# Dilated heads: values for four heads at once with tokens on partitions, and a head's outputs issued behind the gate's tile

## What is computed

```python
qb = rope(qb.reshape(B, S, hb, HEAD_DIM))          # hb = 3 groups * 4 heads
kb = rope(kb.reshape(B, S, hb, HEAD_DIM))
vb = vb.reshape(B, S, hb, HEAD_DIM)
yb = dilated_mixture(qb, kb, vb).reshape(B, S, W_B_OUT) * jax.nn.silu(zb)
# dilated_mixture: causal attention for each group with its window and dilation,
#   (128, 1), (512, 4), (2048, 16), and over the groups a softmax of their log-sum-exps:
w = jax.nn.softmax(jnp.stack(lses, axis=0), axis=0)
out = jnp.sum(w[..., None] * jnp.stack(outs, axis=0), axis=0)
```

## Time and profile before

| | |
|---|---|
| three runs | 3171.05, 3172.30, 3174.02 us (median 3172.3) |
| the profiled execution | 3171.53 us, of which its span 3170.1 us |
| TensorE busy | 3104.5 us, 98% of the span |
| VectorE busy | 1994.0 us, 63% |
| ScalarE busy | 1282.7 us, 40% |
| mean granted TensorE clock | 0.995 |
| dilated stage | from about 2350 to 2592 us of the span |

### The profile page before, as it was taken

The page is one execution under the profiler, slowest core; times in us unless marked ns, Lnnn a source line. Parts: engine busy times, 40 slices in busy tenths (PEclk is TensorE's granted clock), DMA queues, the critical chain, the costliest instruction groups (busy, mean ns, idle before and its releaser), DMA issues.

```text
span 3170.1 us, 47439 instructions
## 1 busy us (share of the span) xinstructions
PE 3104.5 (98%) x19672; PEld 2742.8 (87%) x19672; DVE 1994.0 (63%) x3330; ACT 1282.7 (40%) x1854; POOL 0.2 (0%) x4
## 2 busy tenths in 40 slices
PE   8999999999999999999999999999999999999998
PEld 6677788888888888888878889988999999999998
DVE  5543466757666676575757577768776665555555
ACT  4443323232322323232236465556554444444443
POOL 0000000000000000000000000000000000000000
PEclk9999999999999999999999999999999999999999
DMA  9854533434434344343423234436555555555564
GB/s 370 305 204 179 196 123 120 159 120 134 139 115 152 112 153 146 113 145 120 148 87 113 93 114 153 143 130 216 178 171 182 169 165 174 181 195 195 189 197 149
DMA packets 154645, 511.02 MB, mean 161 GB/s; under 512 B 15552, under 2 KB 36160, under 8 KB 153664
## 3 DMA queue, kind: packets, MB, share of 16 engines
q1 hardware_dynamic: 149904, 495.13, 46.8%
q10 hardware_dynamic: 4528, 12.86, 1.1%
HBM read 503.72 MB, written 4.21 MB: 160 GB/s over the span
## 4 chain that ended last, share of the span: by engine, by line
PE 90%; DVE 5%; ACT 3%; DMA 1%; issue 1%; ACTq 0%; DVEq 0%
PE bank L641 29%; PE bank L643 28%; PE bank L642 28%; DVE w_lo L1772 1%; PE bank L703 1%; DMA raw<-stream 1%; PE bank L921 1%; ACT w_hi L1168 1%; ACT a_s L1478 1%; PE bank L867 0%; DVE a_s L2208 0%; DVE a_numbers L2218 0%; ACT a_s L1420 0%; ACT a_pt L1491 0%; PE bank L881 0%
## 5 line engine op out<-in xcount | busy, mean ns | idle before, releaser
L641 PE MATMUL bank<-h_hi,w_hi 128*128 128x256 f32 (+1 forms) x4032 | 1255.7, 311 | 9.3 <-DVE w_lo L1772 4.6
L643 PE MATMUL bank<-h_hi,w_lo 128*128 128x256 f32 (+1 forms) x4032 | 1240.6, 308 | 0.0
L642 PE MATMUL bank<-h_lo,w_hi 128*128 128x256 f32 (+1 forms) x4032 | 1240.3, 308 | 0.0
L1772 DVE TENSOR_TENSOR w_lo<-raw,w_hi 128x1024 fp32r<-128x1024 f32 x729 | 882.2, 1221 | 417.1 <-ACT w_hi L1168 414.5
L1168 ACT ACTIVATE w_hi<-raw 128x1024 fp32r<-128x1024 f32 x729 | 761.8, 1056 | 890.1 <-PE bank L643 781.1
L641 PEld LDWEIGHTS bank<-h_hi,w_hi 128*128 128x128 f32 x4032 | 760.5, 189 | 66.5 <-issue 21.4
L642 PEld LDWEIGHTS bank<-h_lo,w_hi 128*128 128x128 f32 x4032 | 760.6, 189 | 46.2 <-issue 3.4
L643 PEld LDWEIGHTS bank<-h_hi,w_lo 128*128 128x128 f32 x4032 | 760.4, 189 | 43.0
L641 PE MATMUL bank<-w_hi,h_hi 128*128 128x512 f32 x704 | 284.0, 403 | 12.8 <-DVE w_lo L1772 5.9
L643 PE MATMUL bank<-w_hi,h_lo 128*128 128x512 f32 x704 | 276.1, 392 | 0.0
L642 PE MATMUL bank<-w_lo,h_hi 128*128 128x512 f32 x704 | 275.7, 392 | 0.0
(11 more groups left out here) (274 smaller groups left out, 3058.8 us busy)
## 6 DMA issues: line engine op xcount, KB each, us to landing
raw<-stream SPq DMA_DIRECT2D x904, 512.0 KB, 4.1
raw_h<-stream SPq DMA_DIRECT2D x32, 512.0 KB, 10.4
res<-tokens_in ACTq DMA_DIRECT2D x4, 1024.0 KB, 8.9
vg<-mem_in ACTq DMA_DIRECT2D x4, 512.0 KB, 8.7
c_rows<-cond_rows SPq DMA_DIRECT2D x4, 512.0 KB, 4.3
h_hi<-mem_kv ACTq DMA_DIRECT2D x2, 1024.0 KB, 10.0
out<-res SPq DMA_DIRECT2D x4, 512.0 KB, 3.0
mem_kv<-qk ACTq DMA_DIRECT2D x1, 1024.0 KB, 8.5
```

Source lines behind the costliest of these rows:

```text
L641: pe.matmul(out, sh, mh, start=start, stop=False, **checks)
L642: pe.matmul(out, sh, ml, start=False, stop=False, **checks)
L643: return pe.matmul(out, sl, mh, start=False, stop=stop, **checks)
L1772: dve.tensor_tensor(in_quarters(m.low(raw)[:, :]), m.raw[SLOT[raw]], in_quarters(m.w_hi[slot][:, :]).bitcast(F32), ALU.subtract).then_inc( ...
```

## The change

The values of the dilated branch are made with `values_chunk` before the first dilated head, for each of the three groups, with tokens on partitions and the four heads side by side in 512 columns. ScalarE copies the six banks into six buffers `d_v`, of which four are buffers of earlier stages. The tiles `di_v`, the transposes, the copies of both and the waits for them go away. On TensorE the outputs of head h-1 come behind the tile `di_z` instead of behind `di_q`. On ScalarE and VectorE the programs of a head lose the calls for `di_v` and keep the rest of their order.

```diff
@@ stream_order
     at_b = 4 * W_A
+    for n in range(N_DIL):
+        for c in range(8):
+            values(("dv", n), "w_in_2", at_b + 2 * W_B + n * W_B_OUT, c)
     for h in range(DIL_HEADS):
-        for name, part in (("di_k", 1), ("di_q", 0), ("di_v", 2)):
+        for name, part in (("di_k", 1), ("di_q", 0)):
@@ Memory
+        self.d_v = [self.rstd, *self.sq, self.sq_sum, sb("d_v4", [P, W_B_OUT]),
+                    nc.alloc_sbuf_tensor_at("d_v5", [P, W_B_OUT], F32, offset=tab_at)]
@@ tensor_program
     def dilated_outputs(h):
-        causal_outputs(("di", h), [[m.b_v[:, n, t, :] for t in range(2)] for n in range(3)])
+        pe.wait_ge(*banks.at("dv", N_DIL - 1, 1))
+        causal_outputs(("di", h), [[m.d_v[2 * n + t][:, h * P:(h + 1) * P] for t in range(2)] for n in range(3)])
...
+    for n in range(N_DIL):
+        outs = values_banks(("dv", n), 2)
+        for c in range(8):
+            values_chunk(("dv", n), outs, c)
     for h in range(DIL_HEADS):
...
         for n in range(3):
             tile(("di_q", h, n), LAT)
+        tile(("di_z", h), LAT)
         if h:
             dilated_outputs(h - 1)
-        for n in range(3):
-            tile(("di_v", h, n), LAT)
-        tile(("di_z", h), LAT)
-        pe.wait_ge(*banks.at("di_v", h, 2))
-        for j0, k in ((0, 2), (2, 1)):
-            out = bank("di_vt", h, j0)
-            for j in range(k):
-                for t in range(2):
-                    at = (j * 2 + t) * P
-                    mm = pe.transpose(out[:, at:at + P], m.raw_v[:, j0 + j, t * P:(t + 1) * P], ident)
-            mm.then_inc(*s["mv_turned"].up("di", h, j0))
         pe.wait_ge(*s["roped"].at("di_q", h))
-        pe.wait_ge(*banks.at("di_vt", h, 2))
         causal_scores(("di", h), [(m.b_q[:, n, :], m.b_k[:, n, :]) for n in range(3)])
@@ scalar_program
+    for n in range(N_DIL):
+        for c in range(8):
+            weights_to(WHERE["dv", n][c])
+        act.wait_ge(s.mm, DONE[WHERE["dv", n][7]])
+        for t in range(2):
+            act.activation(m.d_v[2 * n + t][:, :], psum("dv", n, t)[:, :], ACT.Copy).then_inc(*banks.up("dv", n, t))
     for h in range(DIL_HEADS):
...
         swap(("di_q", h), m.q_swp, m.b_q, 64, banks.at("di_q", h, 2))
         if h:
             dilated_outputs(h - 1)
-        for n in range(3):
-            ahead(("di_v", h, n))
         if h:
             act.wait_ge(*s["y_lo"].at("di", h - 1))
...
         tanh(("di_z", h), m.b_g[:, 0, :])
-        for j0, k in ((0, 2), (2, 1)):
-            act.wait_ge(*s["mv_turned"].at("di", h, j0))
-            act.activation(m.b_v[:, j0:j0 + k, :, :],
-                           psum("di_vt", h, j0)[:, 0:k * L].rearrange("p (j t c) -> p j t c", t=2, c=P), ACT.Copy
-                           ).then_inc(*banks.up("di_vt", h, j0))
@@ vector_program
+    for n in range(N_DIL):
+        for c in range(8):
+            weights_to(WHERE["dv", n][c])
     for h in range(DIL_HEADS):
...
         if h:
             dilated_back(h - 1)
-        for n in range(3):
-            scaled_in(("di_v", h, n), m.raw_v[:, n, :], 1.0)
         silu(("di_z", h), m.b_g[:, 0, :])
-        dve.wait_ge(*s["mv_turned"].at("di", h, 2))
```

More of the change, by code:

```diff
@@ L385 @@
     "cond_act", "cond_done", "cond_rows", "modded", "mod1_set", "dve_step", "act_step", "tables_set", "ada_turned",
-    "bias1", "squared", "sq_sum", "meaned", "rstd", "h_raw", "h_mod", "h_hi", "h_lo", "mv_turned",
+    "bias1", "squared", "sq_sum", "meaned", "rstd", "h_raw", "h_mod", "h_hi", "h_lo",
     "swapped", "roped", "q_hi", "q_lo", "s_hi", "s_lo", "v_hi", "decay_arg", "decay_exp", "decay", "tanh", "gate", "scored", "weighed",
@@ L542, in __init__ @@
         self.x2_rstd = sb("b_x2_rstd", [P, 2])
+        tab_at = v_lo_at[1] - 4 * TABLES_N - (v_lo_at[1] - 4 * TABLES_N) % 32
+        self.d_v = [self.rstd, *self.sq, self.sq_sum, sb("d_v4", [P, W_B_OUT]),
+                    nc.alloc_sbuf_tensor_at("d_v5", [P, W_B_OUT], F32, offset=tab_at)]
         self.b_k, self.b_q = self.res[:, 3:6, SIDE], self.res[:, 0:3, SIDE]
@@ L549, in __init__ @@
         self.q_swp = self.b_s[:, 0, :].rearrange("p (a b) -> p a b", b=L)
-        self.raw_v = self.b_s[:, 1, :].rearrange("p (a b) -> p a b", b=L)
         self.h_t2 = [self.b_s[:, j // 3, j % 3 * L:(j % 3 + 1) * L] for j in range(6)]
```

## The result

The changed kernel takes 3176.8 us (median of 22 executions, 3172.1 to 3182.3) against 3172.0 us of the kernel before (22 executions, 3168.0 to 3174.6). The ratio is 1.0016 with a 95% interval of 1.0009 to 1.0022: 4.8 us longer, a difference clear of the noise (2.9 to 7.0 us by the interval). Forecast were 3177.6 us, 5.3 us above the median that was known then. The profiled execution is one of the short ones, 3173.1 us.

The account below looks back on a forecast made before the run. TensorE, busy 98% of the span, was taken as the bound; +1.1 - 6.4 - 0.1 + 8.1 + 3.4 = +6.1 us on the profiled execution's 3171.53 us gave 3177.6 us, range (8 in 10) 3172.0 to 3181.0.

Parts of the forecast that it names:

- Part 1: Values' matmuls on TensorE: 576 of 256 columns removed (65.3 us), 288 of 512 added (66.3 us), sum +1.1 us.
- rival of cheap wide matmuls: 512-column matmuls run at half the trace row's time, saving some 28 us: 3150 us; chance 1%.
- Part 2: End of each dilated head: transposes and TensorE's wait for their copies go, -6.4 us; merged float32 groups about -0.1 us.
- Part 3: Less cover between di_q and the scores: rotated queries still in time, head 0 waits 0 to 0.1 us, taken as 0.
- Part 4: Late weight splits and softmax behind the scores: TensorE stalls 2.2 us in heads 1 and 2, 3.7 behind head 3, +8.1 us.
- Part 5: Clock falls from 2.4 to 1.2 GHz behind the long wait and one of two short ones: +3.4 us, between 0 and 5.1.
- the cover: Rival: weight chunks arrive in time behind the scores, no stalls, -5.4 us, 3166.1 us; chance 10%.
- case of three falls: All three gaps in heads 1 to 3 bring the low clock, 3 x 1.7 us: 3179.3 us; chance about 25%.
- Head 0 had room enough: Rival: head 0 stalls too, having just 0.7 us of room, or waits reach further: +2 to +5 us, 3180 to 3183; 7%.

Follow-up runs that it names:

- e6: Kernel before without the 24 value transposes and ScalarE's copies of them (dilated outputs are other numbers): 3164.1 us against 3171.4, ratio 0.9979.
- e7: Changed kernel with unread matmuls ahead of TensorE's three waits, those in heads 1 and 2 without the start flag: 3175.9 us.
- e8: The changed kernel itself, run again on the chip of the kernel with unread matmuls: 3178.2 us (3171.4 to 3181.0).
- e10: Changed kernel with outputs back behind di_q and the next two chunks' splits placed in idle times of ScalarE and VectorE: 3166.6 us against 3171.2, ratio 0.9984.
- e1: Changed kernel with the chunks behind di_z split ahead of head h-1's outputs on ScalarE and gating on VectorE: 3166.7 us against 3171.8, ratio 0.998.
- e9: Three more traces of the changed kernel, nothing altered: stage from last moba scores to first memory scores 273.71, 275.69 and 275.66 us.
- e5: Changed kernel with the early split of the chunks behind di_z on ScalarE alone: 3170.9 us against 3171.4, ratio 0.9998.

## Why the prediction was right

The forecast was a shade slower, for a stated reason, and both the time and the reason held. By its steps:

- **Part 1** (values' matmuls), +1.1 us: measured 66.54 against 65.3 us, +1.2 us. A matmul of 512 columns costs within 2% of two of 256 (0.2303 against 0.2267 us). The rival of cheap wide matmuls falls. The Trainium skill's 131 ns ("TensorE: Matmul & The Clock Gate", "Back-to-back issue gap") are not what these operands take, 230 ns; the section doesn't say for which type they stand. In the rival's price the prediction mixed two rates: half the row's rate would save 32 us, and 28 us is what the page's figure gives.
- **Part 2** (transposes), -6.4 us and -0.1: e6 gives -6.8. The rest, some 0.1 us a head, lies in the scores: in the kernel before they come behind a wait, and L881 follows L875 by 0.74 to 0.75 us; in e6 by 0.66 us. The -0.1 us for the merged groups was not measured by itself.
- **Part 3** (cover of the rotation), no wait: right for heads 1 to 3, where the scores start at 7.52 (forecast 7.5). In head 0 they are 0.26 us late: the rotation ended 5.76 us behind the last matmul of di_q, and not 5.4 us as in head 1, from which it was read. The prediction had named 0 to 0.1 us and taken 0.
- **Part 4** (stalls), 2.2, 2.2 and 3.7 us: the waits shown are 1.97, 1.97 and 3.56 us (the shown wait is less by what the matmul ahead still runs). Head 0 has none. The chain held link by link: counted from the last matmul of di_q (it starts at 2490.07, 5.56 us ahead of the outputs), gating at 7.72, splits at 9.09, masks at 12.79, exponentials at 15.82, k4 used at 19.82; forecast were 7.71, 9.1, 12.8, 15.85 and 19.9. (For the masks the prediction took off 0.3 us where its row had a wait of 0.24; measured are the 1.40 us that it came to.) The stage as a whole grew by 3.0 us, where parts 1 to 4 sum to 2.7; head 0's late scores are most of the rest.
- **Part 5** (clock), +3.4 us: the mechanism was right, the certainty was not. I took the fall behind the long wait as given; in one of five executions, the first trace, there is none, and the cost of one ran from 1.5 us (the mean of a trace with three) to 2.65 us. On average two of three waits brought it, which is the number that I used, and over the five traces the falls cost 3.3 us. That is close to the term, with some luck: "one of the two" short waits was chosen between two rows of one trace, and five traces don't fix the odds. Of the first comparison's medians 4.8 - 3.0 = 1.8 us are left for the clock; beside e7 the median was longer (3178.2 against 3171.4 us, 3.8 us left). So the term was too large for the one set and about right for the other.
- **The sum**: its terms give +6.1 us. The forecast of +5.3 us came from adding them to one execution that happened to lie 0.8 us below the median of three. That shift says nothing of the change, and it brought the number nearer to the measured 4.8 us: this is luck. Against +6.1 us the change cost 1.3 us less, within the interval of 2.9 to 7.0 us.
- **The rivals**: the cover didn't hold. The case of three falls is real: three of the five traces show it, at 3178.5, 3175.9 and 3178.4 us where it was given 3179.3. Its deciding question, whether gaps of 2.0 us count like that of 1.97 or like that of 2.02 us, was put wrongly, since either wait goes now one way, now the other. The first comparison's median lies below that case, e8's comes near it. Head 0 had room enough.

What the gain would have been is shown by e10 and e1: the idea of the change is worth 5 us (0.16 to 0.2%), and the order in which it was threaded into the other engines cost 7.4 us in the stage (8.3 us against e10), and the clock's part on top.

## What to carry to other kernels

When a tile is taken out of one engine's stream, look in the other engines' programs for what was hung on that tile: here the call that split the next weights went away with it, and the next such call stood behind a wait that TensorE's reordering had made later. Follow the chain from that wait through each in-order queue to the next thing that the busy engine needs, row by row. On an engine that is 98% busy, price a new idle gap with what the clock may add, and judge such a change by a median over many executions, since one trace may show none of that.

## What the runs showed of the hardware

- The fall of the clock behind an identical wait is a matter of the execution: in the changed kernel's five traces it came behind waits of 1.97 us in 3 of 5 each, behind that of 3.56 us in 4 of 5, at 1.6 us a fall in e8 and 2.65 us in the first trace of e9. Under it 40 to 50 matmuls run in 7 us instead of 60 to 62.
- Over all 14 traces, behind three waits ahead of the stage: 14 of 14 (3.07 to 3.11 us), 10 of 14 (1.97 to 2.01 us), 3 of 14 (2.02 to 2.03 us).
- Waits of 0.76, 0.77 and 2.35 us (e5) had a clock of 1.00 in the 7 us behind them in the one trace, and the mean clock of its executions was 0.9947, that of the kernel before on the same chip 0.9946.
- A wait can hide: head 0's scores start 0.26 us late in a row that has no bracket. The distance of the starts shows it.
